# Wide multiplications in four FFNs and z units between the levels of two mixers

## What is computed

```python
def swiglu(x, w_gate, w_up, w_down):                   # FFNs 0 to 3, D_FF = 2816
    return (jax.nn.silu(x @ w_gate) * (x @ w_up)) @ w_down

# the mixer: 6672 columns of projections of h = rmsnorm(x)
(qkv, z, beta_r, a_r, hq, hf_fwd, hf_bwd, hi, hgate, gate_dn, gate_hg) = _split(h @ w_in, IN_SIZES)
# gated delta rule over q, k, v (needs the inverse of a + I per chunk), both directions
o_dn = _gated_rmsnorm(o_f + o_b, z, dn_norm)           # ... * silu(z)
o_hg = _gated_rmsnorm(o_hf + o_hb, hgate, hg_norm)     # HGRN2 scan of hq, hf, hi
merged = (jax.nn.sigmoid(gate_dn) * (o_dn @ w_branch_dn)
          + jax.nn.sigmoid(gate_hg) * (o_hg @ w_branch_hg))
return merged @ w_out
```

## Time and profile before

| | |
|---|---|
| median of 3 runs | 2311.51 us (2311.47 to 2316.66) |
| the profiled execution | 2303.78 us, span of its instructions 2301.6 us |
| granted TensorE clock, mean | 0.988 |
| busy: TensorE, VectorE, ScalarE, GpSimd | 2184.7, 1566.2, 1064.4, 191.6 us |
| weight units | 324 of 1 MB, median 4.8 us from issue to landing |

### The profile page before, as it was taken

The page is one execution under the profiler, slowest core; times in us unless marked ns, Lnnn a source line. Parts: engine busy times, 40 slices in busy tenths (PEclk is TensorE's granted clock), DMA queues, the critical chain, the costliest instruction groups (busy, mean ns, idle before and its releaser), DMA issues.

```text
span 2301.6 us, 39173 instructions
## 1 busy us (share of the span) xinstructions
PE 2184.7 (95%) x15722; PEld 2038.9 (89%) x15722; DVE 1566.2 (68%) x2330; ACT 1064.4 (46%) x1504; POOL 191.6 (8%) x157
## 2 busy tenths in 40 slices
PE   7999989999999999999998998999999998999997
PEld 7998859989999998798997988898998988898996
DVE  4557657656575575667556689867767689867676
ACT  4335465533353345554333475434434475434442
POOL 0000000131000000000001007300000007300000
PEclk9999999999999999999999999999999999999999
DMA  6554424475555554344553442214554442214553
GB/s 251 188 182 165 165 74 165 153 214 184 208 194 187 188 191 146 128 147 166 185 191 139 165 147 92 74 56 149 190 189 167 165 147 92 74 62 168 183 183 126
DMA packets 52665, 359.10 MB, mean 156 GB/s; under 512 B 6400, under 2 KB 6784, under 8 KB 11072
## 3 DMA queue, kind: packets, MB, share of 16 engines
q1 hardware_dynamic: 46928, 340.81, 41.3%
q0 software_dynamic: 4336, 13.37, 2.1%
q10 hardware_dynamic: 1280, 3.19, 0.4%
HBM read 356.29 MB, written 1.05 MB: 155 GB/s over the span
## 4 chain that ended last, share of the span: by engine, by line
PE 79%; DVE 11%; ACT 4%; DMA 4%; issue 2%; SPq 0%; DVEq 0%; POOLq 0%; ACTq 0%
PE tile L754 43%; PE acc L787 18%; PE tile L767 7%; PE tile L1078 3%; DMA ring<-weights 3%; DVE ring_lo L1813 2%; PE tile L1269 2%; ACT w_hi L1340 2%; PE tile L923 1%; PE tile L897 1%; PE tile L802 1%; DVE work L2332 1%; DVE work L2303 1%; DVE bn L2198 0%; DVE work L2301 0%
## 5 line engine op out<-in xcount | busy, mean ns | idle before, releaser
L1813 DVE TENSOR_TENSOR ring_lo<-ring,w_hi 128x1024 fp32r<-128x1024 f32 x648 | 788.6, 1247 | 594.1 <-ACT w_hi L1340 591.9
L1340 ACT ACTIVATE w_hi<-ring 128x1024 fp32r<-128x1024 f32 x648 | 657.7, 1053 | 913.8 <-DMA ring<-weights 706.2
L754 PE MATMUL tile<-xT_hi,w_hi 128*128 128x256 f32 x3008 | 859.3, 286 | 25.7 <-DVE xT_lo L1804 13.9
L754 PE MATMUL tile<-xT_lo,w_hi 128*128 128x256 f32 x3008 | 854.2, 284 | 0.0
L754 PE MATMUL tile<-xT_hi,ring_lo 128*128 128x256 f32 x3008 | 854.0, 284 | 0.0
L754 PEld LDWEIGHTS tile<-xT_hi,w_hi 128*128 128x128 f32 x3008 | 580.3, 193 | 33.7 <-DVE ring_lo L1813 17.0
L754 PEld LDWEIGHTS tile<-xT_lo,w_hi 128*128 128x128 f32 x3008 | 580.5, 193 | 2.1
L754 PEld LDWEIGHTS tile<-xT_hi,ring_lo 128*128 128x128 f32 x3008 | 580.2, 193 | 0.0
L787 PE MATMUL acc<-w_hi,hidden_hi 128*128 128x512 f32 x528 | 206.6, 391 | 2.0 <-DVE ring_lo L1813 2.0
L787 PE MATMUL acc<-w_hi,hidden_lo 128*128 128x512 f32 x528 | 206.1, 390 | 0.0
L787 PE MATMUL acc<-ring_lo,hidden_hi 128*128 128x512 f32 x528 | 205.5, 389 | 0.0
(11 more groups left out here) (273 smaller groups left out, 2718.1 us busy)
## 6 DMA issues: line engine op xcount, KB each, us to landing
ring<-weights SPq DMA_DIRECT2D x324, 1024.0 KB, 4.8
work<-ln_g_rows POOLq DMA_DIRECT2D x8, 512.0 KB, 6.0
work<-ln_b_rows POOLq DMA_DIRECT2D x8, 512.0 KB, 7.2
work<-rpb POOLq DMA_DIRECT2D x32, 96.0 KB, 13.7
x<-x_in SPq DMA_DIRECT2D x1, 1024.0 KB, 8.0
work<-mem_in ACTq DMA_DIRECT2D x1, 1024.0 KB, 6.6
out<-x POOLq DMA_DIRECT2D x1, 1024.0 KB, 4.4
work<-hmask_in ACTq DMA_DIRECT2D x1, 840.0 KB, 8.3
```

What stands on the lines that cost most here:

```text
L754: j = mm(ps[:, f * S:(f + 1) * S], w[a][:, k, :], x2[b][:, k, :], start=(k == 0 and i == 0), stop=(k == KT - 1 and i == 2))
L1340: A(high_of(u, h), half_of(ring, u, h), ACT.Copy).then_inc(sems["w_hi"], 1)
L1813: V.tensor_tensor(half_of(ring_lo, u, h), half_of(ring, u, h), high_of(u, h).bitcast(F32), ALU.subtract).then_inc(sems["w_lo"], 1)
```

## The change

FFNs 0 to 3 (`two_tiles`): `xT_lo` and `xT_hi` become two halves of one tensor, `xT_parts`. A gate/up unit takes two tiles, one for each half. Per k tile one matmul of the high weights has both parts of x as its moving operand (two runs of 256 columns, 512 together), and one of the low weights adds the high x to the first 256 columns. The two column halves of a tile must then be added: ScalarE copies the first, VectorE adds the second from PSUM, for gate (in `hidden`) and for up (in `up_low`); the Silu then reads SBUF.

Mixers: hi is followed at once by the l2 and decay sums, hz by level 0. z 0 is projected after the gate halves of level 2, z 1 after those of level 5; the weight stream is packed in the new order. z is taken by a Copy, and one Silu over both z tiles stands in the last inverse step ahead of the Sigmoid; GpSimd's gains for z go behind its last masks. `near_start` moves from k = 2 to k = 3, so behind that level's gather; the near row behind (3, 0) moves behind z 1. On VectorE the arguments of level 1 go behind the weights fed at hz 1.

```diff
 PROJECTED = (("qkv", 0), ("hf", 0), ("qkv", 1), ("hf", 1), ("qkv", 2), ("hf", 2), ("qkv", 3), ("hf", 3),
              ("qkv", 4), ("hq", 0), ("qkv", 5), ("hq", 1),
-             ("hi", 0), ("hi", 1), ("hz", 0), ("hz", 1), ("z", 0), ("z", 1))
+             ("hi", 0), ("hi", 1), ("hz", 0), ("hz", 1))
...
-NEAR_AFTER_HALF = ((3, 0), (3, 1), (4, 0), (4, 1), (5, 0), (5, 1), (6, 0), (6, 1), (7, 0))
+Z_AT = {2: 0, 5: 1}
+NEAR_AFTER_Z = (5,)
+NEAR_AFTER_HALF = ((3, 1), (4, 0), (4, 1), (5, 0), (5, 1), (6, 0), (6, 1), (7, 0))
+
+
+def two_tiles(n):
+
+    return n < 4
...
+            def features_wide(u, t, x_set=None, more=0):
+
+                for f in range(2):
+                    high, low = open_half(u, f, KT, more)
+                    ps = open_tile(t + f, 2 * more)
+                    for k in range(KT):
+                        if x_set is not None and f == 0 and k % 2 == 0:
+                            await_x(x_set, k // 2)
+                        mm(ps[:, :], high[:, k, :], xT_parts[:, :, k, :], start=(k == 0), stop=False)
+                        j = mm(ps[:, 0:S], low[:, k, :], xT_hi[:, k, :], start=False, stop=(k == KT - 1))
+                    j.then_inc(sems["unit_used" if f else "half_used"], 1)
+
...
-                for name in ("hi", "hz"):
-                    for j in range(2):
-                        project(name, j)
+                for j in range(2):
+                    project("hi", j)
                 square_sums()
                 decay_sums()
                 for j in range(2):
-                    project("z", j)
+                    project("hz", j)
...
+                    if k in Z_AT:
+                        project("z", Z_AT[k])
+                    if k in NEAR_AFTER_Z:
+                        near_row(next(rows))
...
-                        act.wait_ge(sems["unit_used"], more * 6 + plan.ready[t0 + f][1])
-                        src = bank[(t0 + f) % NB][:, 0:S]
+                        t = t0 + 2 * f
+                        act.wait_ge(sems["half_used"], more * 6 + plan.ready[t][1])
+                        A(hidden[:, f % 4, :], bank[t % NB][:, 0:S], ACT.Copy).then_inc(sems["small_out"], 1)
+                        act.wait_ge(tile_taken[t % NB], more * 2 + t // NB + 1)
+                        src = hidden[:, f % 4, :]
                     A(hidden[:, f % 4, :], src, ACT.Silu).then_inc(sems["gate_silu"], 1)
+
+                def up_small(f, more):
+
+                    t = t0 + 2 * f + 1
+                    act.wait_ge(sems["unit_used"], more * 6 + plan.ready[t][1])
+                    A(up_low[:, f % 2, :], bank[t % NB][:, 0:S], ACT.Copy).then_inc(sems["small_out"], 1)
...
                 for j in range(2):
-                    feed_one("z", j)
-                    silu_tokens(T[("z", l, j)], tok2(zs, j))
+                    feed_one("hz", j)
+                    silu_tokens(T[("hz", l, j)], tok2(hz, j))
...
+                    if k in Z_AT:
+                        feed_one("z", Z_AT[k])
+                        t = T[("z", l, Z_AT[k])]
+                        take(t, tok2(zs, Z_AT[k]), lambda ps: ps.rearrange("p (t c) -> p t c", t=TT))
...
                     if v == LEVELS - 1:
+                        for j in range(2):
+                            act.wait_ge(*taken(T[("z", l, j)]))
+                        A(zs, zs, ACT.Silu).then_inc(sems["z_silu"], 1)
                         for i in range(8):
                             act.wait_ge(*taken(T[("gate", l, i)]))
                         A(gates[:, :, :], gates[:, :, :], ACT.Sigmoid).then_inc(sems["gates_ready"], 1)
...
+                def gate_sum(f, more):
+
+                    t, h = t0 + 2 * f, f % 4
+                    ps = bank[t % NB]
+                    dve.wait_ge(sems["small_out"], more * 8 + 2 * FT * n + 2 * f + 1)
+                    V.tensor_tensor(hidden[:, h, :], hidden[:, h, :], ps[:, S:2 * S], ALU.add).then_inc(tile_taken[t % NB], 1)
+
+                def up_sum(f, more):
+
+                    t = t0 + 2 * f + 1
+                    ps = bank[t % NB]
+                    dve.wait_ge(sems["small_out"], more * 8 + 2 * FT * n + 2 * f + 2)
+                    V.tensor_tensor(up_low[:, f % 2, :], up_low[:, f % 2, :], ps[:, S:2 * S], ALU.add).then_inc(tile_taken[t % NB], 1)
+                    dve.wait_ge(tile_taken[t % NB], more * 2 + t // NB + 1)
...
                         feed(u0 + m, more, halves=(0,))
                     if f is not None and conv_first:
                         convolve(n, f, more)
+                    if f is not None and two_tiles(n):
+                        gate_sum(f, more)
                     if m + 2 < FU:
                         feed(u0 + m, more, halves=(1,))
+                    if f is not None and two_tiles(n):
+                        up_sum(f, more)
                     if f is not None:
                         product(f, more)
...
                 feed_one("hi", 1)
                 next(parts)
-                feed_one("hz", 0)
-                next(parts)
-                feed_one("hz", 1)
-                args(l, 1)
-
                 t = T[("gcum", l)]
...
-                feed_one("z", 0)
+                next(parts)
+                feed_one("hz", 0)
                 for j in range(4):
                     dve.wait_ge(sems["l2_inv"], 4 * l + j + 1)
                     V.tensor_tensor(pair(qkvT, j), pair(qkvT, j), pair(l2s, j), ALU.mult).then_inc(sems["l2_done"], 1)
-                feed_one("z", 1)
+                feed_one("hz", 1)
+                args(l, 1)
...
                         if half == 0 and k < LEVELS:
                             args(l, k + 2)
-                        if half == 1 and k == 2:
+                        if half == 0 and k == 3:
                             near_start()
...
                 row_gains("hz", hz, 1)
                 qmul(6)
-                row_gains("z", zs, 0)
                 qmul(7)
                 qmul(8)
                 level_masks(NEAR + 1)
                 level_masks(NEAR + 2)
+                row_gains("z", zs, 0)
```

More of the change, by code:

```diff
@@ L130, in ffn @@
             if c == "G":
+                if two_tiles(name[1]):
+                    self.ready.append(("half_used", self.units))
+                    self.tiles += 1
                 self.ready.append(("unit_used", self.units))
@@ L387, in weight_stream @@
         out += [packed[name][j:j + 1] for name, j in PROJECTED]
-        out.append(pack_features(w[:, 4624:6672]))
+        gates = pack_features(w[:, 4624:6672])
+        for k in range(8):
+            out.append(gates[k:k + 1])
+            if k in Z_AT:
+                out.append(packed["z"][Z_AT[k]:Z_AT[k] + 1])
         out.append(pack_branch(a["w_branch_hg_2"][l]))
@@ L505, in build @@
         col = sb("col", [P, cols.shape[1]])
+        up_low = None
         bn = sb("bn", [P, 4, 6])
@@ L1686, in mixer2 @@
                 i.then_inc(sems["hg_qs"], 1)
[L1687 to L1691 removed]
+                feed_one("hi", 0)
+                silu_qkv(5)
                 act.wait_ge(sems["qkv_silu"], 6 * l + 4)
```

59 lines of the change are left out of this document (37 added, 22 removed).

## The result

The changed kernel takes 2317.56 us (median; 2311.8 to 2328.9) beside 2311.2 us of the kernel before in the same comparison (2304.35 to 2316.77). The ratio is 1.003, interval 1.002 to 1.0041: 6.4 us slower, where the forecast was 2290.5 us, 21 us faster, with a range of 2281 to 2302. Sign and range were both wrong.

The account below looks back on a forecast made before the run. TensorE was taken to bound the FFNs, with TensorE and VectorE waiting for each other in the mixers. FFNs -18 and each mixer -3.0 - 0.8 + 2.3 = -1.5 made -21 us, from 2311.5 to 2290.5; range 2281 to 2302.

Parts of the forecast that it names:

- What bounds the kernel: Whole kernel: TensorE alone bounds the four first FFNs; in the mixers' levels TensorE and VectorE wait for each other in turn.
- the slower rival: FFNs: hand-overs between ScalarE and VectorE bound them, +25 us in place of -18, 2333.5 us; chance 0.05.
- Part 1, the price of a pair: Gate/up units of four FFNs: 1408 trios become pairs, each 11.9 to 13.6 ns cheaper; 18 us taken.
- the two-run operand: Wide matmuls: moving operand of two 256-column runs 8 KB apart, costed at nothing; upper bound half speed, +280 us.
- Part 2, level 0 earlier: First mixer: with z moved from ahead of it, level 0 begins 10.8 us earlier.
- z 0: Behind level 2's gates: its 5.8 us find 5.0 us of idle time and cost 0.3 to 0.8.
- The strided sums: Third gather: four VectorE sums of 3.85 us move behind it, delay the first near step, and VectorE has caught up.
- the mixers lose: Rival: levels gain nothing because near steps come late behind the sums, tail costs 3.6 us; 2300.7 us, chance 0.16.
- z 1: Behind level 5's gates: 5.8 us of work meet 1.64 and 0.8 us of idle time and cost 4 to 5.
- The levels' end: Mixers: the levels end 3 to 4 us earlier, 3.0 taken for each mixer.
- Part 3, the tail: Last inverse level: z's Silu, 1.05 us, and a second table load, 1.28, add 2.3 us per mixer, bounds 0 and 3.6.
- The sum: Whole kernel: FFNs -18 us, both mixers -3 us, together -21 us, giving 2290.5 us.

Follow-up runs that it names:

- wide_only: The kernel before with only the wide form in the first four FFNs, mixers unchanged: 2308.68 us, ratio 0.9979 to the kernel before.
- wide_grouped: wide_only with each half's 8 matmuls of 512 columns first, then the 8 of 256, not in turn: 2301.9 us, ratio 0.9942 to the kernel before.
- wide_adjacent: wide_only with the high and low part of a k tile side by side, so the 512-column operand is one run: 2308.23 us.

## Why the prediction was wrong, step by step

**What bounds the kernel**: right. The FFNs are TensorE's, and the hand-overs that the slower rival feared cost nothing (TensorE 135.60 of 135.60).

**Part 1, the price of a pair.** This step failed. The saving of 12 to 13.6 ns for a matmul left out was worked out from sequences of one width, and applied to an alternation of two, which no row showed; the forecast bounded the two-run operand, which cost nothing, and not the alternation. In place of 346 to 348 ns the steady laps hold 353.8, 8 us in all instead of 18. In the grouped order the price by the forecast's chain rows is right (347.8 ns, measured 348): laps of 16.61 us for 16.6, 15 us by 42 laps and 13.4 in the median; the 18 us took the middle between these rows and the other pair's 346.4 ns. The rule of the Trainium skill, "TensorE: Matmul & The Clock Gate" (Wait — 56ns, not 53.3ns?), some 2.5 ns for each matmul, would give 3.5 us. wide_only's 3.9 are near it by accident: its laps show 8, and the 13.4 of wide_grouped are out of its reach.

**Part 1, the clock.** Not in the sum. With the wide form, its matmuls in turn, the executions of wide_only have a lower mean granted clock (0.9808 for 0.9835), worth about the 4 us between laps and median.

**Part 2, level 0 earlier**: right, 11.1 us for 10.8 in the first mixer; in the second 9.7.

**z 0**: right. At the start of gate unit 3 the first mixer is 1413.21 after 1338.29, and was 1424.22 after 1340.34: 9.0 us ahead, for 7.5 to 8 (6.9 in the second mixer). The wait at the transposes fell from 5.03 to 0.60.

**The strided sums.** This step failed: "VectorE has caught up". It had not, since its hole lay ahead of the gather, and the 3.84 us of sums came out as TensorE's waits: 3.8 to 3.9 us in each mixer by the table, 6.8 us in the medians. The 5.03 us wait had one cover to spend and got two, z 0 and the move. The rival "the mixers lose" names this very mechanism and was given 0.16.

**z 1**: 4 to 5 us were forecast. In the first mixer gate unit 5, ahead of z 1, starts 5.0 us earlier than before, relative to hi, and gate unit 6, behind it, 0.3 later: z 1 cost 5.4 us, and 5.3 in the second mixer.

**The levels' end**: 3.0 us earlier were forecast, and 0.2 / 1.5 later came. With the sums ahead of the gather it is 3.6 / 2.4 earlier.

**Part 3, the tail.** Silu and second table load: right, 2.4 us. "VectorE's stretch under GpSimd is hidden by the same wait" held only while that wait was there; without it, it was 1.4 us of its own (1.74 to 0.34). Too low was the size: the tail is 4.6 / 3.8 us longer, above the bound of 3.6. In the first mixer the rest is the clock behind the wait (0.50): for it the bound had 1.3 us, and the way from there to dn_o is 2.4 us longer. In the second the clock behind the wait was 1.00, and the rest is the low clock around hg_T. wide_adjacent, with the mixers of before, has that too (its tail there is 21.15 us), so this part of the 3.8 needn't be the change's.

**The sum.** -18 became -3.9 and -3 became +8.2. No rival alone gives that: the mixers' loss was larger than its worst case (+7.2), and the loss of the wide form came together with it. The forecast took the rivals one at a time, each against a sum otherwise right; that made the range too narrow at the top. The base did no harm, since the sum was set against the median too.

## What to carry to other kernels

Price a matmul by rows of the very sequence that will run: a long and a short matmul in turn had two steady rates, and one inner loop split in two turned -3.9 into -13.4 us. Give a wait one cover: before a step is moved out of a wait, look where its engine is idle once the first cover is in place. Keep long ScalarE operations and table loads behind the last take that TensorE waits for; 2.4 us more of waiting cost up to 4.6, where the clock fell behind it.

## What the hardware showed beyond that

- The mixed sequence slows its neighbours too: down units of unchanged matmuls took 5.50 us in laps with pairs of 353.8 ns, and 5.47 with grouped ones.
- One unchanged kernel was busy at 1.2 GHz for 32 us in one execution and for 58 in another.
- TensorE came back from six waits of 3.15 or 3.16 us at one place at granted clocks of 0.50, 1.00, 0.69, 0.69, 0.69 and 0.50 over the next 5.5 us, and from 26 waits of 1.75 us or less at 1.00.
- Of the Trainium skill, "ScalarE: Activation LUTs" (What ACT_TABLE_LOAD costs), the drain of 1.38 us is not seen here either: the Silu starts 0.01 us after its load ended, the Sigmoid 0.01 us after the second.
